# The output stage's orders, and head 0 of the expert retrieval by token tile with four modulation pieces on TensorE

## The chip, the cores and the metric

The kernel runs on one core of one Trainium2 chip. The metric is the device time of one execution in microseconds (us). The core has TensorE (PE in the rows, its weight loads PEld), VectorE (DVE), ScalarE (ACT), GpSimd (POOL) and SyncE (SP). Here SP issues the direct loads of weights and POOL the gathers and the loads of `w_ada`; 16 DMA engines carry both.

## The reference, cut to what matters

All in float32, 256 tokens of width 2048 (two token tiles of 128):

```python
mod = silu(c) @ w_ada + b_ada                 # w_ada: 2048 x 12288, six parts of 2048
sh1, sc1, g1, sh2, sc2, g2 = split(mod, 6)
...                                           # attention: stick-breaking heads and latent heads
mixed = concat(norm(sb_out), norm(mla_out)) @ w_o
x = x + g1 * mixed
h2 = rmsnorm(x, norm2_g) * (1 + sc2) + sh2
q = h2 @ w_peer_q                             # 8 heads, two halves of 128 each
s1, s2 = q1 @ keys1.T, q2 @ keys2.T           # 128 scores a side, for each token and head
v1, i1 = top_k(s1, 16); v2, i2 = top_k(s2, 16)
best, pos = top_k(v1[:, None] + v2[None, :], 16)   # 16 experts of 16384
u, v = take(u_tab, expert), take(v_tab, expert)    # rows of 2048 numbers
x = x + g2 * sum(softmax(best) * gelu(u . h2) * v) # sum over 8 heads and 16 experts
return rmsnorm(x)
```

## The kernel before, in words

The kernel is written by hand: each engine has one program (`@block.tensor` and so on) that runs in its written order, and semaphores order the engines among each other. Memory is placed by hand too: `at(name, offset, shape)` puts a buffer at an address, and buffers whose lives don't overlap share one.

**Modulation.** `w_ada` comes in 96 pieces `k` of 1 MB (part `k // 16`, chunk `k % 16`). From piece 32 on POOL loads them (`ada_load`, L279) into three buffers `ada_late` in turn; each load waits until the piece that was in its buffer is summed. VectorE adds piece times `silu(c)` to `ada_acc` (`ada_sum`, L293). When the 16 pieces of a part are in, `ada_cols(part)` (L304) sums over the 128 partitions with 16 TensorE products that have one column each, and `ada_finish` adds the bias. The last three pieces go to buffers of their own (`ada_last`), which are loaded once the squares of the new `x` are done (`x2_squared`), ahead of pieces 89 to 92.

**Output stage.** `w_o` has four column groups `n`, each in 8 pairs `m` of chunks. For a pair ScalarE casts the weights to a high part (L416), VectorE makes the low part (L420), and TensorE runs 12 products of 512 columns (L927), the two token tiles `t` alternating. VectorE's list between these casts holds `ada_sum` of pieces 71 to 85, the residual sums, and in the last group the additions L1598 to L1607. `ada_cols(4)` stands behind pair 5 of group 2 on TensorE; the sum of piece 80 (pair 6) waits for it. Ahead of the stage ScalarE waits for the sums of squares of all 16 heads (L1233).

**Second norm and head 0.** x is normed, transposed (L946) and evicted to `h2T`. Then TensorE computes the queries `p{u}` of head `u` for both tiles at once: 32 products of 256 columns (L981), with weights `w_pq{u // 2}` from two slots (`ring`) of which each half is loaded when its last reader is done. `score(u)` (L958) makes the scores, ScalarE evicts them to `s_all`, and VectorE's `retrieve(part, q)` takes 17 parts to find the 16 experts of job `q` (token tile `q // 8`, head `q % 8`). `token_rows(u)` (L967) transposes `h2T` back to rows `h2`. `ada_cols(5)` stands in head 2 behind pair 5.

**Experts.** There are 256 slots `n` (job `n // 16`). POOL gathers for each slot a row of `peer_u` per token (1 MB) into seven `u_rows`, and later, between them, a row of `peer_v` into nine `v_rows`. VectorE's `serve(n)` is the product `dot(n)` (L1740) and, behind it, a share of the retrieval of a later job: jobs 1 and 2 over slots 0 to 7 and 8 to 15, then job `q + 2` over the 16 slots of job `q`. TensorE sums the `v_rows` in PSUM (L1012). What holds the first gathers, in POOL's order:

```python
if n % TOPK == 0: pool.wait_ge(experts_ready, n // TOPK + 1)
if n < 3:   pool.wait_ge(ada_steps, LAST_PIECES - EARLY)           # buffers of ada_late
elif n < 6: pool.wait_ge(ada_steps, LAST_PIECES - EARLY + n - 2)   # buffers of ada_last
if n == 6:  pool.wait_ge(ada_columns, 4)                           # ada_acc, after ada_cols(5)
```

From slot 7 on a gather of `u` waits for the product seven slots back. The gather of `v` 0 waits for `p5` and that of `v` 4 for `p7`, whose weights lay where the `v_rows` are.

## Time and profile before

| | us |
|---|---|
| median of 3 runs | 1834.54 (1834.16 to 1836.43) |
| the profiled execution | 1835.33 |
| its span in the trace | 1832.7 |
| TensorE, busy | 1473.0 (80%) |
| VectorE, busy | 1141.4 (62%) |
| ScalarE, busy | 349.0 (19%) |
| GpSimd, busy | 619.3 (34%) |

The page splits the span into 40 slices of 45.8 us. Experts fill it from slice 12 on. Times in the rows are us from the start of the span. Matmuls in float32 show as two records each, so that "x32" at L304 is 16 products.

### The profile page before, as it was taken

The page shows a single profiled execution, that of the slowest core. Times are in us where ns is not written, and L with a number is a line of the kernel's source. Part 1 is how long each engine was busy: PE and PEld are TensorE (multiplying, and loading weights), DVE is VectorE, ACT ScalarE, POOL GpSimd, SP SyncE. Part 2 cuts the span into 40 slices and gives each one's busy share as a digit, 9 for nine tenths or more (in the row PEclk, how much of TensorE's full clock was granted, in tenths as well). Part 3 has the DMA queues.
Part 4 walks back from the last instruction along what each step waited for, and adds up shares of the span by engine and source line. Part 5 has one row for each costly group of instructions (what it writes and reads, how often), then busy time and mean ns, then how long its engine had stood idle before and what let it go on. Part 6 is the DMA issues. An engine that isn't in the chain of part 4 may idle for free.

```text
span 1832.7 us, 13707 instructions
## 1 busy us (share of the span) xinstructions
PE 1473.0 (80%) x4834; PEld 829.5 (45%) x4834; DVE 1141.4 (62%) x1562; ACT 349.0 (19%) x697; POOL 619.3 (34%) x625
## 2 busy tenths in 40 slices
PE   2979999899898987777777777778777777777776
PEld 2559986887787632232322323224332322232332
DVE  5868786788789855545455555538555555544445
ACT  3004342852301211011110100102111101010110
POOL 0001111001064863444334343418543443433341
PEclk9989999999999999999999999998999999999999
DMA  9999998569799999999999999999999999999995
GB/s 340 386 388 405 400 353 313 204 238 384 273 360 413 421 422 421 422 422 422 422 421 422 422 422 421 422 421 404 421 422 423 422 422 422 422 422 421 422 421 233
DMA packets 138241, 716.43 MB, mean 391 GB/s; under 512 B 11158, under 2 KB 15436, under 8 KB 63692
## 3 DMA queue, kind: packets, MB, share of 16 engines
q0 software_dynamic: 82976, 604.02, 79.8%
q1 hardware_dynamic: 55212, 111.77, 16.6%
q8 instruction: 25, 0.41, 0.1%
q14 instruction: 28, 0.23, 0.0%
HBM read 713.65 MB, written 2.10 MB: 391 GB/s over the span
## 4 chain that ended last, share of the span: by engine, by line
DMA 60%; PE 18%; DVE 11%; POOL 5%; issue 3%; ACT 2%; SPq 1%; DVEq 0%; POOLq 0%; ACTq 0%
DMA u_rows<-in_peer_u,expert 49%; PE ps L981 4%; PE ps L768 4%; DMA v_rows<-in_peer_v,expert 4%; DVE u_rows L1740 3%; DVE first_acc L454 3%; POOL v_rows L665 3%; DMA ring<-in_w_peer_q 2%; PE ps L762 2%; POOL u_rows L665 2%; DMA ada_first<-in_w_ada 2%; PE ps L927 2%; DMA ada_late<-in_w_ada 2%; DVE ada_acc L293 1%; DMA u_rows<-in_peer_v,expert 1%
## 5 line engine op out<-in xcount | busy, mean ns | idle before, releaser
L1012 PE MATMUL ps<-v_rows,diag 128*128 128x512 f32 x1960 | 902.5, 606 | 271.5 <-DMA v_rows<-in_peer_v,expert 257.4
L1740 DVE SCALAR_TENSOR_TENSOR u_rows<-u_rows,h 128x2048 f32<-128x2048 f32 x256 | 587.0, 2293 | 519.8 <-DMA u_rows<-in_peer_u,expert 517.3
L1012 PEld LDWEIGHTS ps<-v_rows,diag 128*128 128x128 f32 x1960 | 357.5, 191 | 815.1 <-issue 586.3
L665 POOL DMA_INDIRECT u_rows<-in_peer_u,expert x256 | 286.0, 1117 | 620.9 <-DVE u_rows L1740 574.8
L665 POOL DMA_INDIRECT v_rows<-in_peer_v,expert x249 | 285.3, 1146 | 97.3 <-issue 78.3
L1339 ACT ACTIVATE diag<-ident,hidden 128x128 f32<-128x128 f32 x250 | 89.3, 395 | 846.8 <-PE ps L1012 532.9
L293 DVE SCALAR_TENSOR_TENSOR ada_acc<-ada_late,cact,ada_acc 128x2048 f32<-128x2048 f32 x57 | 133.9, 2349 | 18.2 <-DMA ada_late<-in_w_ada 17.1
L279 POOL DMA_DIRECT2D ada_late<-in_w_ada x61 | 32.3, 530 | 314.1 <-DVE ada_acc L293 268.3
L981 PE MATMUL ps<-h2T,ring 128*128 128x256 f32 x512 | 117.5, 390 | 6.4 <-DMA ring<-in_w_peer_q 6.4
L981 PEld LDWEIGHTS ps<-h2T,ring 128*128 128x128 f32 x512 | 99.4, 196 | 20.8 <-DMA ring<-in_w_peer_q 6.8
L454 DVE SCALAR_TENSOR_TENSOR first_acc<-ada_first,cact,first_acc 128x1024 f32<-128x1024 f32 x60 | 77.0, 1284 | 15.1 <-DMA ada_first<-in_w_ada 9.6
L732 PE MATMUL ps<-opened,hT 128*128 128x512 f32 (+1 forms) x128 | 53.5, 581 | 5.8 <-DVE hT L1447 5.8
L420 DVE TENSOR_TENSOR ring_low<-ring,win_high 128x1024 fp32r<-128x1024 f32 x40 | 48.0, 1220 | 13.4 <-ACT win_high L416 13.3
L416 ACT CAST win_high<-ring 128x1024 fp32r<-128x1024 f32 x40 | 41.6, 1051 | 74.7 <-DMA ring<-in_w_in 39.3
L927 PE MATMUL ps<-wo_high,mix_high_part 128*128 128x512 f32 x128 | 42.1, 411 | 7.3 <-DVE ring_low L420 7.2
L927 PE MATMUL ps<-wo_high,mix_low_part 128*128 128x512 f32 x128 | 41.7, 409 | 0.0
L646 POOL MEMSET kpad<- 128x512 f32 x1 | 0.5, 524 | 120.7 <-DVE a1c L1409 120.7
L732 PEld LDWEIGHTS ps<-opened,hT 128*128 128x128 f32 x128 | 26.9, 214 | 30.6 <-issue 26.2
L420 DVE TENSOR_TENSOR ring_low<-ring,wo_high 128x1024 fp32r<-128x1024 f32 x32 | 39.0, 1220 | 2.1 <-ACT wo_high L416 2.1
L416 ACT CAST wo_high<-ring 128x1024 fp32r<-128x1024 f32 x32 | 33.5, 1048 | 31.7 <-PE ps L927 31.7
L1287 ACT ACTIVATE hidden<-hidden 128x16 f32<-128x16 f32 x16 | 3.5, 216 | 173.1 <-DVE u_rows L1740 173.0
L927 PE MATMUL ps<-ring_low,mix_high_part 128*128 128x512 f32 x128 | 35.5, 401 | 0.0
(273 smaller groups left out, 1262.6 us busy)
## 6 DMA issues: line engine op xcount, KB each, us to landing
ada_late<-in_w_ada POOLq DMA_DIRECT2D x61, 1024.0 KB, 7.9
ada_first<-in_w_ada SPq DMA_DIRECT2D x64, 512.0 KB, 11.6
ring<-in_w_in SPq DMA_DIRECT2D x10, 2048.0 KB, 25.6
ring<-in_w_o SPq DMA_DIRECT2D x8, 2048.0 KB, 20.5
ring<-in_w_peer_q SPq DMA_DIRECT2D x8, 2048.0 KB, 14.4
opened<-in_w_in SPq DMA_DIRECT2D x8, 1024.0 KB, 12.8
u_rows<-in_peer_u,expert POOLq DMA_INDIRECT x256, 32.2
v_rows<-in_peer_v,expert POOLq DMA_INDIRECT x249, 34.2
```

What stands on the lines that cost most here:

```text
L293: nc.vector.scalar_tensor_tensor(out=a, in0=piece, scalar=cact[:, kc:kc + 1], in1=a, op0=ALU.mult, op1=ALU.add).then_inc(ada_steps, 1)
L416: nc.scalar.copy(self.high, self.whole).then_inc(made, 1)
L420: nc.vector.tensor_tensor(self.low, self.whole, self.high.bitcast(F32), ALU.subtract).then_inc(done, 1)
L454: nc.vector.scalar_tensor_tensor(out=a, in0=piece, scalar=cact[:, kc:kc + 1], in1=a, op0=ALU.mult, op1=ALU.add).then_inc(first_steps, 1)
L665: nc.gpsimd.indirect_dma_start(buf[:, :], None, table, bass.IndirectOffsetOnAxis(ap=expert[:, q, k:k + 1], axis=0)).then_inc(done, 16)
L732: ins = nc.tensor.matmul(banks[name][t][:, 0:width], hT[:, ch, P * t:P * t + P], w[:, ch % 4, 0:width], start=(ch == 0), stop=last)
L768: ins = nc.tensor.matmul(banks[b // 2][:, T * (b % 2):T * (b % 2) + T], w.of(part, k, P * b, P), h[:, ch, :], start=first and b % 2 == 0, ...
L927: ins = nc.tensor.matmul(banks[t], mixed[:, h, P * t:P * t + P], w.of(part, k), start=first, stop=last)
L981: ins = nc.tensor.matmul(bank[:, T * s:T * s + T], ring[item[name][0]][:, lo:lo + P], h2T[:, ch, :], start=(ch == 0 and s == 0), stop=(ch ...
L1012: ins = nc.tensor.matmul(ps[:, c, :], diag[i % len(diag)][:, :], buf[:, 512 * c:512 * c + 512], start=(n % HALF_SLOTS == 0), stop=last)
L1339: nc.scalar.activation(diag[i % len(diag)][:, :], ident[:, :], ACT.Copy, scale=hidden[:, q % 4, k:k + 1]).then_inc(diagonal, 1)
L1740: nc.vector.scalar_tensor_tensor(out=buf[:, :], in0=buf[:, :], scalar=1.0, in1=h2[:, q // H, :], op0=ALU.mult, op1=ALU.mult, accum_out=hid ...
```

## The change

1. **Orders of the output stage.** ScalarE's load of the activation table ahead of attention moves up behind the copies `uq`. The wait for all sums of squares ahead of the output stage goes; the casts of `mix` wait each for its own heads, the last for the sums. VectorE's first step on these sums moves behind pair 1. `ada_cols(4)` moves from behind pair 5 to behind pair 3 of group 2. The last pair runs tile 0 and then tile 1.
2. **Head 0 by token tile.** `first_head(t)` computes the queries of one tile with tokens as rows: 16 products of 256 columns. They are copied to `q0`, transposed (`first_turned`), copied and scored (`first_score`), so that VectorE can retrieve job 0 when tile 0 alone is scored.
3. **Four pieces on TensorE.** `ada_last` has four buffers (pieces 92 to 95) on one semaphore. They are not summed by VectorE: `last_piece(i)` multiplies each with its column of `silu(c)` right into the PSUM columns of part 5. `ada_cols(5)` adds the rest to them and moves to the end of head 1.
4. **Buffers and retrievals.** `u_rows` 0 to 2 lie where `ada_last` 1 to 3 were, 3 to 5 at `ada_late`, 6 at `ada_acc`; the waits of the first gathers follow. VectorE retrieves job 0 behind the sum of piece 88, waits until POOL has issued the first gather, then sums pieces 89 to 91. Job 2 and all later ones are spread over 16 slots from slot 8 on.

```diff
-    LAST_PIECES = 6 * KC - 3
+    LAST_PIECES = 6 * KC - 4
+    def last_piece(i):
+        if i == 0:
+            nc.tensor.wait_ge(ada_last_loaded, 16 * len(ada_last))
+        k = LAST_PIECES + i
+        part, kc = divmod(k, KC)
+        for b in range(KC):
+            ins = nc.tensor.matmul(ps[:, 7, KC * part + b:KC * part + b + 1], ada_last[i][:, P * b:P * b + P],
+                                   cact[:, kc:kc + 1], start=(i == 0 and b == 0), stop=False, skip_group_check=True)
+        ins.then_inc(ada_columns, 1)
...
                 if n < 3:
-                    pool.wait_ge(ada_steps, LAST_PIECES - EARLY)
+                    pool.wait_ge(ada_columns, 5 + n)
                 elif n < 6:
-                    pool.wait_ge(ada_steps, LAST_PIECES - EARLY + n - 2)
+                    pool.wait_ge(ada_steps, LAST_PIECES - EARLY - 5 + n)
                 if n == 6:
-                    pool.wait_ge(ada_columns, 4)
+                    pool.wait_ge(ada_columns, 8)
...
+                    if w.c == 4 * PAIRS - 1:
+                        for t in range(TT):
+                            for p in products:
+                                product(*p, t)
...
-                    if n == 2 and m == 5:
+                    if n == 2 and m == 3:
                         ada_cols(4)
...
+            first_head(0, 0, KC)
+            first_head(1, 0, 3)
+            first_turned(0)
+            first_head(1, 3, 6)
+            first_score(0)
+            first_head(1, 6, KC)
+            last_piece(0)
+            first_turned(1)
+            last_piece(1)
+            first_score(1)
+            last_piece(2)
+            last_piece(3)
+            for u in range(4):
+                token_rows(u)
-            for u in range(H):
+            for u in range(1, H):
...
-                    if u == 2 and m == 5:
+                    if u == 1 and m == 7:
                         ada_cols(5)
...
-            act.wait_ge(squares_summed, JOBS)
             for n in range(4):
                 for m in range(PAIRS):
                     if n == 0:
+                        copied(act, f"o{4 * m + 2 if 2 * m < H else 4 * m + 3 - 2 * H}")
+                        if m == PAIRS - 1:
+                            act.wait_ge(squares_summed, JOBS)
...
-                job, slots = (1 + k // 8, 8) if q == 0 else (q + 2, TOPK)
+                job, slots, k2 = (1, 8, n) if n < 8 else (2 + (n - 8) // TOPK, TOPK, (n - 8) % TOPK)
...
-            for k in g2_steps[:-3]:
+            for k in g2_steps[:3]:
                 ada_sum(k)
             for part in range(RETRIEVAL):
                 retrieve(part, 0)
-            for k in g2_steps[-3:]:
+            dve.wait_ge(first_issued, 1)
+            for k in g2_steps[3:-4]:
                 ada_sum(k)
```

TensorE's order from the transposes of the second norm on, before: head 0 in one (32 products), its rows and scores, head 1, and `ada_cols(5)` (L304) in head 2.

```order
L946 MATMUL ps<-ident,xs_116 128x128 x32
L981 MATMUL ps<-h2T,ring_49 128x256 x32
L967 MATMUL ps<-ident,h2T 128x128 x4
L958 MATMUL ps<-kT,pq 128x128 x4
L967 MATMUL ps<-ident,h2T 128x128 x12
L981 MATMUL ps<-h2T,ring_49 128x256 x32
L981 MATMUL ps<-h2T,ring_50 128x256 x4
L958 MATMUL ps<-kT,pq 128x128 x4
L981 MATMUL ps<-h2T,ring_50 128x256 x20
L304 MATMUL ps<-ones,ada_acc 128x1 x16
```

The same place now; L317 is `last_piece`.

```order
L969 MATMUL ps<-ident,xs_117 128x128 x32
L1003 MATMUL ps<-ring_49,h2T 128x256 x19
L1012 MATMUL ps<-ident,q_188 128x128 x2
L1003 MATMUL ps<-ring_49,h2T 128x256 x3
L1019 MATMUL ps<-kT,pq 128x128 x2
L1003 MATMUL ps<-ring_49,h2T 128x256 x10
L317 MATMUL ps<-cact,ada_last_88 128x1 x16
L1012 MATMUL ps<-ident,q_188 128x128 x2
L317 MATMUL ps<-cact,ada_last_89 128x1 x16
L1019 MATMUL ps<-kT,pq 128x128 x2
L317 MATMUL ps<-cact,ada_last_90 128x1 x16
L317 MATMUL ps<-cact,ada_last_91 128x1 x16
```

Four times 16 products with one column stand now between head 0 and the token rows, and with them ahead of head 1.

POOL's order from the loads of `ada_last` to the eighth gather, with the waits, before:

```order
L279 DMA ada_last_88<-in_w_ada 128x2048 [waits x2_squared]
...
L665 DMA u_rows_134<-in_peer_u,expert 128x2048 [waits ada_steps,experts_ready]
L665 DMA u_rows_135<-in_peer_u,expert 128x2048 [waits ada_steps]
L665 DMA u_rows_136<-in_peer_u,expert 128x2048 [waits ada_steps]
...
L665 DMA u_rows_140<-in_peer_u,expert 128x2048 [waits ada_columns]
L665 DMA u_rows_134<-in_peer_u,expert 128x2048 [waits dots]
```

and now:

```order
L281 DMA ada_last_88<-in_w_ada 128x2048 [waits x2_squared]
...
L679 DMA u_rows_135<-in_peer_u,expert 128x2048 [waits ada_columns,experts_ready]
L679 DMA u_rows_136<-in_peer_u,expert 128x2048 [waits ada_columns]
L679 DMA u_rows_137<-in_peer_u,expert 128x2048 [waits ada_columns]
...
L679 DMA u_rows_141<-in_peer_u,expert 128x2048 [waits ada_columns]
L679 DMA u_rows_135<-in_peer_u,expert 128x2048 [waits dots]
```

The first three gathers wait no longer for VectorE's sums but each for one `last_piece` on TensorE.

## Rows read from the trace of the kernel before

**Rows 1.** The page: rate of the DMA engines in 40 slices.

```profile
GB/s 340 386 388 405 400 353 313 204 238 384 273 360 413 421 422 421 422 422 422 422 421 422 422 422 421 422 421 404 421 422 423 422 422 422 422 422 421 422 421 233
```

**Rows 2.** Stretches: window, length, busy us (PE, PEld, DVE, ACT, POOL), clock, DMA share, GB/s.

```profile
500.00:505.00 5.00, 5.00 (x26) 4.44 (x25) 4.33 (x19) 0.59 (x1) 0.00 (x0) 1.00 0.01 3
505.00:510.00 5.00, 5.00 (x25) 4.40 (x24) 4.39 (x16) 0.00 (x0) 0.00 (x0) 1.00 0.19 59
...
520.00:600.00 80.00, 73.58 (x356) 64.69 (x355) 73.57 (x134) 10.22 (x19) 43.78 (x29) 0.91 1.02 415
```

**Rows 3.** Timeline of POOL, first and seventh gather; idle before and releaser in brackets.

```profile
510.84 2.88 POOL L665 DMA_INDIRECT u_rows<-in_peer_u,expert  x1 [17.42 <-DVE expert L1713]
...
529.98 0.94 POOL L665 DMA_INDIRECT u_rows<-in_peer_u,expert  x1 [5.81 <-PE ps L304]
```

**Rows 4.** Timeline of TensorE: head 0, and from head 1 into head 2.

```profile
481.38 14.05 PE L981 MATMUL ps<-h2T,ring 128*128 128x256 f32 x64
...
500.25 15.71 PE L981 MATMUL ps<-h2T,ring 128*128 128x256 f32 x72
```

**Rows 5.** Timeline of VectorE: three sums, start of retrieval 0, first product.

```profile
482.36 7.25 DVE L293 SCALAR_TENSOR_TENSOR ada_acc<-ada_late,cact,ada_acc 128x2048 f32<-128x2048 f32 x3
...
500.52 0.29 DVE L1672 MAX8 tk_v<-s_all 128x8 f32<-128x128 f32 x1
...
518.58 2.29 DVE L1740 SCALAR_TENSOR_TENSOR u_rows<-u_rows,h 128x2048 f32<-128x2048 f32 x1 [0.83 <-DMA u_rows<-in_peer_u,expert]
```

**Rows 6.** Chain that ended last: three pairs, `ada_cols(4)`, load of piece 85, `ada_cols(5)`.

```profile
422.89 8.45 PE ps L927 x36
431.34 3.48 PE ps L304 x32
...
443.30 9.12 DMA ada_late<-in_w_ada
...
525.49 4.22 PE ps L304 x32
```

**Rows 7.** Stretches of 1 us (columns as in Rows 2) in and behind these products.

```profile
432.00:433.00 1.00, 1.00 (x12) 1.00 (x11) 0.00 (x0) 1.00 (x2) 0.00 (x0) 1.00 1.05 387
436.00:437.00 1.00, 1.00 (x4) 0.81 (x3) 1.00 (x2) 0.00 (x0) 0.50 (x1) 0.50 1.05 387
527.00:528.00 1.00, 1.00 (x11) 1.00 (x10) 1.00 (x1) 0.00 (x0) 0.00 (x0) 1.00 1.10 440
528.00:529.00 1.00, 1.00 (x7) 1.00 (x6) 1.00 (x3) 0.00 (x0) 0.00 (x0) 0.50 0.88 358
534.00:535.00 1.00, 1.00 (x4) 0.82 (x3) 0.71 (x2) 0.00 (x0) 0.70 (x2) 0.59 0.96 393
```

**Rows 8.** Timelines of VectorE and TensorE in the output stage.

```profile
434.92 1.29 DVE L290 TENSOR_SCALAR ada_acc<-ada_late,cact 128x2048 f32<-128x2048 f32 x1 [4.45 <-PE ps L304]
...
434.67 0.72 PE L927 MATMUL ps<-wo_high,mix_high_part 128*128 128x512 f32 x2
...
438.97 0.76 PE L927 MATMUL ps<-wo_high,mix_high_part 128*128 128x512 f32 x2
...
456.07 0.98 PE L927 MATMUL ps<-wo_high,mix_high_part 128*128 128x512 f32 x2 [2.05 <-DVE ring_low L420]
...
469.55 1.04 PE L908 MATMUL ps<-ident,knat 128*128 128x128 f32 x8
```

**Rows 9.** Timeline of ScalarE: start of attention, start and end of the output stage.

```profile
309.96 1.28 ACT L1205 ACT_TABLE_LOAD   x1
...
360.78 0.62 ACT L1237 CAST mix_high_part<-mix 128x512 fp32r<-128x512 f32 x1 [0.39 <-PE ps L886]
...
472.49 0.63 ACT L1230 ACTIVATE junk<-x 128x512 f32<-128x512 f32 x1 [0.60 <-DVE x L1607]
```

**Rows 10.** Timelines: VectorE at the start of attention; POOL's gather of `v` 4.

```profile
310.83 2.35 DVE L293 SCALAR_TENSOR_TENSOR ada_acc<-ada_late,cact,ada_acc 128x2048 f32<-128x2048 f32 x1 [0.42 <-DMA ada_late<-in_w_ada]
...
619.92 2.42 POOL L665 DMA_INDIRECT v_rows<-in_peer_v,expert  x1 [0.56 <-PE ps L981]
```

More of the change, by code:

```diff
@@ L310, in ada_finish @@
     def ada_finish(part):
-        nc.vector.wait_ge(ada_columns, part - 1)
+        nc.vector.wait_ge(ada_columns, part - 1 if part < 5 else 8)
         lo, hi = KC * part, KC * part + KC
@@ L366, in build @@
     before_retrieval = list(used)
-    plan([f"p{u}" for u in range(8)], [0, 1, 2, 3])
-    plan([f"sc{u}" for u in range(8)], [4, 5])
+    plan(["fq_0", "fq_1", "p0_0", "p0_1"] + [f"p{u}" for u in range(1, 8)], [0, 1, 2, 3])
+    plan(["sc0_0", "sc0_1"] + [f"sc{u}" for u in range(1, 8)], [4, 5])
     plan([f"h2_{u}" for u in range(8)], [6])
@@ L661, in _, with gather @@
                 ada_load(pool, k)
-            def gather(n, buf, done, table):
+            def gather(n, buf, done, table, issued=None):
                 q, k = divmod(n, TOPK)
-                nc.gpsimd.indirect_dma_start(buf[:, :], None, table,
-                                             bass.IndirectOffsetOnAxis(ap=expert[:, q, k:k + 1], axis=0)).then_inc(done, 16)
+                nc.gpsimd.indirect_dma_start(buf[:, :], None, table, bass.IndirectOffsetOnAxis(ap=expert[:, q, k:k + 1], axis=0),
+                                             engine_sem=issued).then_inc(done, 16)
             def gather_u(n):
@@ L968, in token_rows, with first_head, first_turned, first_score @@
                 fill(ins, f"h2_{u}")
-            for u in range(H):
+            w0 = ring[item["w_pq0"][0]][:, :].rearrange("p (kc n) -> p kc n", kc=KC)
+            def first_head(t, lo, hi):
+                if lo == 0:
+                    take(pe, f"fq_{t}")
+                for ch in range(lo, hi):
+                    if t == 0 and ch % 2 == 0:
+                        copied(pe, f"h2T{ch // 2}")
+                    if t == 0 and ch % KH == 0:
+                        loaded(pe, "w_pq0", ch // KH)
+                    ins = nc.tensor.matmul(ps[:, unit[f"fq_{t}"][0], 0:2 * P], h2T[:, ch, P * t:P * t + P], w0[:, ch, 0:2 * P],
+                                           start=(ch == 0), stop=(ch == KC - 1))
+                if hi == KC:
+                    fill(ins, f"fq_{t}")
+            def first_turned(t):
+                copied(pe, f"fq_{t}")
+                bank = take(pe, f"p0_{t}")
+                for s in range(2):
+                    ins = nc.tensor.transpose(bank[:, P * s:P * s + P], q0[:, t, P * s:P * s + P], ident[:, :])
+                fill(ins, f"p0_{t}")
+            def first_score(t):
+                copied(pe, f"p0_{t}")
+                bank = take(pe, f"sc0_{t}")
+                for s in range(2):
+                    ins = nc.tensor.matmul(bank[:, P * s:P * s + P], pq[:, 0, s, P * t:P * t + P], kT[:, H * s, :], start=True, stop=True)
+                fill(ins, f"sc0_{t}")
+            first_head(0, 0, KC)
[13 more added lines that the diff above has]
+            for u in range(1, H):
                 name, bank = f"w_pq{u // 2}", take(pe, f"p{u}")
                 for m in range(PAIRS):
-                    if u == 0:
-                        copied(pe, f"h2T{m}")
                     if u % 2 == 0 and m % (PAIRS // 2) == 0:
@@ L1298, in std, with first_query, first_query_turned, first_scores_out @@
                 nc.scalar.activation(st[:, 2 + t:3 + t], st[:, 2 + t:3 + t], ACT.Sqrt).then_inc(y_std, 1)
-            for u in range(H):
+            def first_query(t):
+                empty(nc.scalar.copy(q0[:, t, :], full(act, f"fq_{t}")[:, 0:2 * P]), f"fq_{t}")
+            def first_query_turned(t):
+                empty(nc.scalar.copy(pq[:, 0, :, P * t:P * t + P], full(act, f"p0_{t}")[:, 0:2 * P].rearrange("p (s t) -> p s t", s=2)),
+                      f"p0_{t}")
+            def first_scores_out(t):
+                if t == 1:
+                    act.wait_ge(ada_columns, 4)
+                empty(nc.scalar.copy(s_all[:, t, 0:2, :], full(act, f"sc0_{t}")[:, 0:2 * P].rearrange("p (s n) -> p s n", s=2)),
+                      f"sc0_{t}")
+            first_query(0)
+            first_query_turned(0)
+            first_scores_out(0)
+            first_query(1)
+            first_query_turned(1)
+            first_scores_out(1)
+            for u in range(4):
+                token_rows_out(u)
+            for u in range(1, H):
                 if u == 4:
@@ L1304, in _ @@
                 query(u)
-                if u == 0:
-                    token_rows_out(0)
                 scores_out(u)
-                if u == 0:
-                    for k in range(1, 4):
-                        token_rows_out(k)
                 if u == 4:
@@ L1719, in retrieve @@
                 t, h = divmod(q, H)
-                if part == 0 and t == 0:
-                    copied(dve, f"sc{h}")
+                if part == 0 and (t == 0 or h == 0):
+                    copied(dve, f"sc{h}" if h else f"sc0_{t}")
                 if part < 8:
@@ L1785, in serve @@
                     ada_finish(5)
-                job, slots = (1 + k // 8, 8) if q == 0 else (q + 2, TOPK)
+                job, slots, k2 = (1, 8, n) if n < 8 else (2 + (n - 8) // TOPK, TOPK, (n - 8) % TOPK)
                 if job < QJOBS:
-                    for part in range(RETRIEVAL * (k % slots) // slots, RETRIEVAL * (k % slots + 1) // slots):
+                    for part in range(RETRIEVAL * k2 // slots, RETRIEVAL * (k2 + 1) // slots):
                         retrieve(part, job)
```

68 lines of the change are left out of this document (35 added, 33 removed).

## The prediction, made before the changed kernel was run

> **What bounds the kernel now.** I read the page's slices first: from slice 12 to the end the DMA engines are full at 421 to 422 GB/s [rows 1]. The 512 gathers of 1 MB (2.49 us each at 421 GB/s) and the late weight loads fill 1300 us without a gap; the stretch 520 to 600 already runs at 415 GB/s [rows 2]. The bytes don't change. So the end moves only by DMA time that was empty and is now used, or was used and is now empty. I read next the stretches just ahead: 3 and 59 GB/s from 500 to 510 [rows 2]. This hole is there because nothing can be issued: POOL sits 17.42 us until the experts of job 0 are found [rows 3], and the next query weights wait for head 1.
>
> Call S the start of head 0's products, 481.4 now [rows 4]. VectorE starts retrieval 0 at S+19.1 and its first product at S+37.2 [rows 5]; POOL has the experts and issues its first gather at S+29.5 and the seventh, held by `ada_cols(5)`, at S+48.6 [rows 3]. The query weights of slot 0 are read half way through head 1, S+18.9+7.0=S+26 [rows 4], so DMA is full again from about S+27.7 and stays so.
>
> **The change part by part.**
>
> *Table load: 0.* Its 1.28 us at 309.96 stand in ScalarE's path [rows 9], but VectorE, which takes the next step, sums a piece until 313.1 [rows 10]; the piece's load covers it. Without this cover it would be worth up to 1.3.
>
> *Wait for the squares: -0.4.* The cast at 360.78 sat 0.39 for TensorE [rows 9]; now it follows ScalarE's own step. The lower bound of the gain is 0, were the new waits as late.
>
> *`ada_cols(4)`: -4.3.* VectorE sat 4.45 for it [rows 8], and the low parts behind were late: TensorE waited 2.05 at 456.07. From 422.89 on TensorE has 13 pairs of 2.82 (8.45 for three), 3.48 for the columns [rows 6] and 1 for eight of the keys' transposes, 41.1 in all. About 1.2 more goes to the half clock behind the columns: 436 to 437 shows it at 0.50 [rows 7], and the pair from 434.67 to 438.97 took 4.3 [rows 8]. So it ends its last pair at 465.2 instead of 469.5 [rows 8]. Ends: -3, if the loads of the pieces, which land 9.1 behind their issue [rows 6], hold VectorE as they did; -6, if small waits within the 8.45 go too.
>
> *Tile 0 first in the last pair: -0.6.* VectorE gets tile 0 six products (1.4) earlier, but ScalarE is behind with the copies of the keys; of its way to the last square only the idle 0.60 ahead of 472.49 goes [rows 9].
>
> Together S comes 5.2 earlier, at 476.2 (ends 3.5 and 7).
>
> *Head 0 by tile.* 32 products cost 14.05, 0.44 each [rows 4]; 16 cost 7.0. Tile 0's queries are there at S+7, turned at S+8.6, scored at S+10.4 and evicted at S+10.9, with three products of tile 1 in each gap to hide the copies. VectorE is done with three sums (7.25) at S+8.3 [rows 5]. Retrieval takes 10.0 (500.5, with POOL released at 510.5 or just behind [rows 3, 5]), so experts are ready at S+21, 8 earlier. That is the gain meant. What is late next? The first gather needs the buffer of `last_piece(1)`, and the second and third those of pieces 2 and 3.
>
> *The pieces on TensorE.* Each is 16 one-column products, as `ada_cols` is: 3.48 at full clock [rows 6]. Tile 1 ends at S+14.8, piece 0 at S+18.3. Then comes the clock. Behind the L304 products at 431.2 it was 0.50 at 436; at 528, with TensorE busy all of every microsecond and 2.7 into the L304 products, it fell from 1.00 to 0.50; 534 to 535, in ordinary products since 529.7, is the first stretch above that again (0.59) [rows 7]. These are the levels 2.4 and 1.2 GHz. The stint that straddled the fall took 4.22 instead of 3.48 [rows 6]: 7 records a us instead of 11 or 12. Four pieces in a row are four such stints, so from the second on I take twice 3.48. Pieces 1, 2 and 3 then end at S+25.3, S+33.2 and S+40.2 (at full clock S+22.1, S+25.8 and S+29.3).
>
> Here a rule of the Trainium skill speaks against my reading: "TensorE: Matmul & The Clock Gate", section "What's actually happening", has the clock set by how busy the engine has been, low by default and full when busy. By it pieces that keep TensorE fully busy stay at full clock. The rows at 527 to 529 speak against it, for a busy engine with one-column products; what it would give is the first rival.
>
> *Behind the pieces.* Token rows 0 to 3, now behind all pieces, take about as long as the 4.8 between head 0 and head 1 now [rows 4], 6 at half clock: S+46. VectorE's first product needs them, so it starts at S+46 instead of S+37. Head 1 takes 14.05 and some 2.5 for the clock: S+62.5. Then `ada_cols(5)`: S+66, and only then POOL's seventh gather, which was issued at S+48.6. And VectorE behind its first product wants the scores of head 1 for retrieval 1; these come in head 2, at about S+71. Before they were there before the first product. POOL's eighth gather needs that one product, its ninth the second: so from S+49 to S+75 VectorE stands.
>
> *What DMA does with it.* Transfers begin some 1.5 behind the issue. Gather 0: S+27.7, just as before. It takes 2.5, then DMA is empty until gather 1 at S+35.6 (5.4 lost) and gather 2 at S+42.6 (4.5). Gathers 2 to 5 last until S+52.6; half a load of query weights comes at S+56.5 (3.9), the next with the end of head 1 at S+64 (2.5). Gathers 6 and 7 follow; from 8 on each waits for a product. A slot costs VectorE 2.3 and an eighth of a retrieval, 3.6, against 2.5 of DMA: some 6 slots lose 1 each before the last query weights fill the holes, less what the queue holds. I take 5 (2 to 10). Sum: 5.4+4.5+3.9+2.5+5=21.
>
> *Retrievals over 16 slots.* Job 2 costs VectorE half as much per slot from slot 8 on (0.6 instead of 1.25). Later in steady state VectorE has room; 0.
>
> *Gather 0 with VectorE silent.* 0.94 instead of 2.88 for its issue [rows 3]; in the times above.
>
> *Sum*, against the profiled execution: 1835.3-5.2+21=1851. It lies 0.8 above the median, within what a chip adds; I leave it.
>
> **The rivals.**
>
> *Full clock* (the rule above). Gathers 0 to 2 at S+24.5, S+28.2 and S+31.8 lose 1.2 and 1.1, the query weights 1.3 and 2.1, VectorE's pace 4; the phase starts 3.1 earlier: 9.7-3.1=+6.6. 1835.3-5.2+6.6=1837. For it: the L304 stint at 431 ran at 1.00 to its end. Against: the one at 525 did not, and these are four times as long.
>
> *Faster: the intended outcome.* At full clock, with TensorE never late behind: the queued gathers and weights bridge VectorE's wait for head 1, nothing is lost from head 1 on but the three first holes (3.6), and the output stage gives 6.6. 1835.3-6.6-3.1+3.6=1829. It decides when head 1's scores come less than some 10 us behind the first product, since POOL has seven buffers. Against it: gather 6 waits for `ada_cols(5)`, at S+52 even then, and is in order ahead of all others.
>
> *Slower still.* TensorE reaches `p7` late and POOL's gather of `v` 4, which waits for it, stands while the queue runs dry; before it waited just 0.56 at S+138.5 [rows 10], so there is little to spare, and `p7` would be some 20 later, at S+160. Priced at 8 more: 1859.
>
> **How the numbers follow.** Forecast 65%, with its own range 1845 to 1858; full clock 17%; faster 11%; slower still 7%. The range that leaves out no more than 2 in 10 runs from 1834 (the full clock with its terms 3 better) to 1858. About 0.2% (3.7 us) is what a measurement of this kernel can tell from no change. Faster by more than that (under 1830.9) has 0.12, within it 0.16, slower 0.72.
>
> **What would show each step.** In the changed profile: S near 476, and TensorE's last L927 product ending near 465. Experts at S+21 and the first gather released not by VectorE's `expert` but by TensorE's L317. Clock 0.50 in the stretches behind the first `last_piece`, and each later piece near 7; at 1.00 and 3.5 the forecast is wrong and the first rival right. The gathers 0, 1, 2 some 7 apart with DMA below 250 GB/s between S+30 and S+42. VectorE idle 20 us behind its first product, released by the eviction of head 1's scores; gather 6 released by L304 near S+66. DMA from S+95 on at 421 as before: any other rate there would upset the whole argument.

## The result, and the profile after

The changed kernel takes **1846.76 us** (median of 5 runs, 1843.04 to 1849.69) against 1834.16 (5 runs, 1833.11 to 1836.43) for the kernel before, measured beside it: **1.0067 times the time, 95% interval 1.0053 to 1.0082**, slower by 12.6 us. The profiled execution of it took 1845.27 us with a span of 1842.9; before, 1835.33 and 1832.7.

The page's slices, first the granted clock of TensorE in tenths, then the rate of the DMA engines:

```profile
PEclk8989999999889999999999999998999999999999
...
GB/s 339 386 390 404 397 351 321 185 265 389 259 288 393 412 421 422 422 422 421 422 422 421 422 421 422 422 422 413 422 422 423 422 422 422 421 422 421 422 422 236
```

Against [rows 1] the slices 10 to 12, counted from 0 (461 to 599 us), are lower: 259, 288 and 393 where 273, 360 and 413 stood. Slice 13 has 412 for 421, and from slice 14 on both kernels move 421 to 423 in all but one slice and the last. So next to nothing was lost in the 1200 us of gathers; it was lost between 484 and 574 us.

TensorE's timeline from the last products of the output stage to head 1's scores (start, length, engine, line, out<-in, count of records, idle before and releaser in brackets):

```profile
474.29 8.39 PE L1003 MATMUL ps<-ring,h2T 128*128 128x256 f32 x38
...
488.80 3.63 PE L317 MATMUL ps<-cact,ada_last 128*128 128x1 f32 x32
...
492.54 5.66 PE L317 MATMUL ps<-cact,ada_last 128*128 128x1 f32 x32
...
499.05 13.65 PE L317 MATMUL ps<-cact,ada_last 128*128 128x1 f32 x64
512.57 1.09 PE L990 MATMUL ps<-ident,h2T 128*128 128x128 f32 x4
...
518.83 15.12 PE L1046 MATMUL ps<-h2T,ring 128*128 128x256 f32 x64
533.78 3.63 PE L306 MATMUL ps<-ones,ada_acc 128*128 128x1 f32 x32
...
539.94 1.86 PE L981 MATMUL ps<-kT,pq 128*128 128x128 f32 x8
```

S, the start of head 0's products, is 474.3 (481.38 before [rows 4]). The first piece takes 3.6 us, the second 5.7, the last two 6.8 each. Head 1 begins at S+44.5; before it began at S+18.9 [rows 4].

POOL's timeline, the gathers that waited:

```profile
499.07 1.00 POOL L679 DMA_INDIRECT u_rows<-in_peer_u,expert  x1 [15.55 <-PE ps L317]
506.15 2.06 POOL L679 DMA_INDIRECT u_rows<-in_peer_u,expert  x1 [6.08 <-PE ps L317]
512.98 0.94 POOL L679 DMA_INDIRECT u_rows<-in_peer_u,expert  x1 [4.77 <-PE ps L317]
...
537.68 0.94 POOL L679 DMA_INDIRECT u_rows<-in_peer_u,expert  x1 [20.05 <-PE ps L306]
```

The experts were there at 495.1, S+20.8. The first gather went out at S+24.8, the second and third each some 7 us later, the seventh at S+63.4. In [rows 3] the first one waited for VectorE's `expert` and the seventh was issued at S+48.6.

VectorE's timeline: the experts, its first product of rows, and its wait for head 1's scores.

```profile
494.96 0.17 DVE L1791 SCALAR_TENSOR_TENSOR expert<-tk_f 128x16 uint32<-128x16 f32 x1
...
519.76 2.29 DVE L1818 SCALAR_TENSOR_TENSOR u_rows<-u_rows,h 128x2048 f32<-128x2048 f32 x1 [12.40 <-ACT h L1339]
...
542.45 0.29 DVE L1750 MAX8 tk_v<-s_all 128x8 f32<-128x128 f32 x1 [20.39 <-ACT s_all L1335]
```

Stretches from S on (columns as in [rows 2]), first of the changed kernel, S+28 to S+100:

```profile
474.00:502.00 28.00, 28.00 (x160) 26.30 (x157) 19.08 (x42) 3.25 (x8) 2.59 (x4) 0.85 0.58 230
502.00:519.00 17.00, 14.97 (x68) 13.77 (x68) 5.16 (x3) 1.75 (x3) 5.80 (x5) 0.50 0.55 196
519.00:534.00 15.00, 15.00 (x68) 13.03 (x66) 2.30 (x2) 0.60 (x2) 0.00 (x0) 0.93 0.82 318
534.00:549.00 15.00, 15.00 (x82) 13.65 (x82) 6.25 (x13) 1.15 (x2) 2.81 (x3) 0.89 0.84 300
549.00:574.00 25.00, 25.00 (x127) 22.24 (x126) 23.80 (x47) 2.93 (x5) 7.11 (x8) 1.00 0.99 368
```

and the same stretches, as seen from S, of the kernel before:

```profile
481.00:509.00 28.00, 26.35 (x133) 22.70 (x132) 25.01 (x43) 4.32 (x8) 2.11 (x4) 1.00 0.52 201
509.00:526.00 17.00, 17.00 (x88) 15.14 (x87) 14.02 (x16) 1.18 (x2) 11.80 (x6) 1.00 1.02 389
526.00:541.00 15.00, 15.00 (x72) 13.30 (x72) 12.84 (x25) 1.17 (x2) 9.80 (x5) 0.77 1.02 415
541.00:556.00 15.00, 15.00 (x77) 13.32 (x76) 14.17 (x30) 1.76 (x3) 8.26 (x7) 1.00 1.02 414
556.00:581.00 25.00, 25.00 (x127) 22.12 (x127) 23.88 (x42) 4.62 (x10) 15.38 (x8) 1.00 1.02 412
```

I turn a rate into **idle** time: the stretch times (1 - rate/421). After: 12.7, 9.1, 3.7, 4.3 and 3.1 us; before: 14.6, 1.3, 0.2, 0.2 and 0.5. With the last 26 us (0.4 and 0.2) that is 33.3 against 17.1, 16.2 us more.

Two lengths within one execution leave out that the output stage starts a few us earlier or later from one execution to the next (418 to 424 us in those profiled). **Stage**: from the product that ends the chain's last long wait, one pair or three ahead of `ada_cols(4)`, to S; in both kernels that is pair 3 of group 2. The chain has it at

```profile
422.19 3.06 PE ps L939 x12
425.25 3.46 PE ps L306 x32
428.71 31.69 PE ps L939 x132
```

so 52.1 us; before, 422.89 [rows 6] to 481.38 is 58.5. **Rest**: from S to the end of the span, 1842.9-474.3=1368.6; before, 1832.7-481.4=1351.3. The change is -6.4 in the stage and +17.3 in the rest (the stage began 0.7 earlier besides), and the 17.3 are the 16.2 us of empty DMA engines and the 1 us of the slice behind (412 for 421).

### The profile page after: what moved, and what is told of

Its sections match the earlier page's. It is cut to its first block, busy times and chain, and to the rows that moved or that the text cites. A ratio compares the mean times of both kernels' runs of the same rounds, so it can differ in the third digit from the quotient of the medians.

```text
span 1842.9 us, 13978 instructions
## 1 busy us (share of the span) xinstructions
PE 1496.9 (81%) x4966; PEld 852.6 (46%) x4966; DVE 1132.1 (61%) x1558; ACT 349.7 (19%) x701; POOL 627.6 (34%) x625
## 3 DMA queue, kind: packets, MB, share of 16 engines
q1 hardware_dynamic: 55212, 111.77, 16.5%
## 4 chain that ended last, share of the span: by engine, by line
DMA 57%; PE 15%; DVE 12%; POOL 9%; issue 4%; ACT 2%; SPq 2%; DVEq 0%; POOLq 0%; ACTq 0%
DMA u_rows<-in_peer_u,expert 47%; POOL u_rows L679 5%; DVE u_rows L1818 4%; POOL v_rows L679 4%; DMA v_rows<-in_peer_v,expert 4%; PE ps L939 3%; DVE first_acc L467 2%; PE ps L776 2%; DMA ring<-in_w_in 2%; PE ps L782 2%; DVE ada_acc L295 1%; DMA ada_first<-in_w_ada 1%; DMA u_rows<-in_peer_v,expert 1%; PE ps L317 1%; PE ps L438 1%
## 5 line engine op out<-in xcount | busy, mean ns | idle before, releaser
L679 POOL DMA_INDIRECT u_rows<-in_peer_u,expert x256 | 289.7, 1132 | 632.8 <-DVE u_rows L1818 561.7
L679 POOL DMA_INDIRECT v_rows<-in_peer_v,expert x249 | 289.9, 1164 | 97.2 <-issue 78.8
L295 DVE SCALAR_TENSOR_TENSOR ada_acc<-ada_late,cact,ada_acc 128x2048 f32<-128x2048 f32 x56 | 131.5, 2348 | 22.2 <-DMA ada_late<-in_w_ada 16.1
L1046 PE MATMUL ps<-h2T,ring 128*128 128x256 f32 x448 | 100.8, 385 | 0.0
L1046 PEld LDWEIGHTS ps<-h2T,ring 128*128 128x128 f32 x448 | 85.6, 193 | 11.4
L433 DVE TENSOR_TENSOR ring_low<-ring,win_high 128x1024 fp32r<-128x1024 f32 x40 | 48.0, 1219 | 13.8 <-ACT win_high L429 13.8
```

Source lines behind the costliest of these rows:

```text
L295: nc.vector.scalar_tensor_tensor(out=a, in0=piece, scalar=cact[:, kc:kc + 1], in1=a, op0=ALU.mult, op1=ALU.add).then_inc(ada_steps, 1)
L433: nc.vector.tensor_tensor(self.low, self.whole, self.high.bitcast(F32), ALU.subtract).then_inc(done, 1)
L679: nc.gpsimd.indirect_dma_start(buf[:, :], None, table, bass.IndirectOffsetOnAxis(ap=expert[:, q, k:k + 1], axis=0), engine_sem=issued).the ...
L1046: ins = nc.tensor.matmul(bank[:, T * s:T * s + T], ring[item[name][0]][:, lo:lo + P], h2T[:, ch, :], start=(ch == 0 and s == 0), stop=(ch ...
```

## The experiments

In three groups on two chips, each beside the kernel before (medians 1835.0, 1835.3 and 1834.5): `e1` to `e4` on one chip, `e5` to `e8` on another, `e9`, `e10` and `a1` on the first again. Ratios are to the kernel before of the same group. Only the third group has the changed kernel in it too. The columns: S of the profiled execution, the rest, the start of head 1's products and of its scores counted from S, and the idle DMA time of the first 126 us from S, as above.

```
                    median  ratio  95% interval     S     rest   head 1 scores  idle
kernel before         -     1         -           481.4  1351.3   18.9   34.4   17.1
changed kernel      1846.8  1.0067 1.0053-1.0082  474.3  1368.6   44.5   65.6   33.3
a1_changed_again    1844.8  1.0053 1.0040-1.0067  474.1  1371.9   45.0   69.4   36.8
e1_orders           1828.5  0.9969 0.9957-0.9981  470.1  1351.7   18.9   34.4   15.6
e2_head0            1851.6  1.0090 1.0075-1.0106  482.4  1368.6   45.2   66.5   34.5
e3_tile_vector      1828.4  0.9963 0.9951-0.9975  475.2  1355.2   21.1   36.6   19.3
e7_tile_five        1828.1  0.9962 0.9949-0.9975  478.8  1351.3   21.0   36.5   16.6
e4_pieces_one       1823.5  0.9940 0.9926-0.9954  474.7  1347.6   22.2   43.4   12.1
e5_pieces_half      1831.4  0.9982 0.9973-0.9991  473.5  1358.3   31.2   55.6   23.0
e9_one_piece        1826.2  0.9952 0.9939-0.9965  477.4  1349.7   25.5   46.7   15.0
e10_pieces_apart    1845.1  1.0063 1.0051-1.0075  472.4  1369.3   30.7   65.8   33.6
e6_retrieve_later   1845.4  1.0049 1.0036-1.0062  475.2  1368.9   44.9   69.3   31.9
e8_cols_early       1842.7  1.0038 1.0023-1.0052  475.6  1364.8   44.6   66.5   29.2
```

Times from S are of one execution each. The rest of the changed kernel differs by 3.3 us between its two profiled executions (1368.6 and 1371.9), so a difference of 3 or 4 us between two rests shows nothing by itself. With the new orders the stage took 52.0 to 52.3 us in all profiled executions but those of `e7_tile_five` and `e9_one_piece` (54.6 and 54.4).

**Do the two parts add up?** The kernel before with the orders alone, and the changed kernel with the orders undone:

```diff
+                    if w.c == 4 * PAIRS - 1:
+                        for t in range(TT):
+                            for p in products:
+                                product(*p, t)
-                    if n == 2 and m == 5:
+                    if n == 2 and m == 3:
                         ada_cols(4)
```

> The kernel before with the output stage's orders alone: the early table load, the wait for the squares put behind the first copies, ada_cols(4) in front of the last two products' pairs, and the last pair by token tile. Head 0, the sums of the pieces and the retrievals stay as before. Theory (two parts that add up: orders gain, head 0 loses): head 0 starts some 6.9 us earlier, as it did in the changed kernel (474.45 for 481.38), and nothing behind it gives that back, so 1834.2 - 6.9 = 1827 us (1826 to 1829). Rival 1 (the earlier start meets transfers that are not there yet, and the DMA queues idle as much longer in head 0 and 1 as the stage got shorter): 1832 to 1835 us. Rival 2 (most of the 6.9 us came only together with the pieces being taken off VectorE): 5.3 us, as I had summed it, or less: 1829 to 1832 us.

> The changed kernel with the output stage's orders undone: head 0 by token tile, the last four pieces on TensorE, the re-placed retrievals. Theory: this part alone carries the whole loss, 17 us in the two profiled executions (9.9 + 6.9) and 19.5 by the medians (12.6 + 6.9): 1851 to 1854 us, with the clock at 0.50 in the pieces as before. Rival (the two parts don't add up: the loss comes only where the earlier start of head 0 leaves too little loaded, so that undoing the orders costs little or nothing): 1844 to 1848 us.

Measured: 0.9969 and 1.0090, that is -5.7 and +16.5 us by the ratios (the medians: -6.5 and +16.6). Together +10 to +11; the whole change gave 1.0067 and, in its second measurement, 1.0053, 12.3 and 9.7 us. They add up, and neither needs the other: the rival in which the orders gain nothing is out, and so is the one in which undoing them costs little (1844 to 1848). TensorE's chain in the orders alone is the changed kernel's:

```profile
418.05 3.01 PE ps L925 x12
421.07 3.46 PE ps L304 x32
424.53 31.67 PE ps L925 x132
457.08 2.75 PE ps L925 x12
```

From 418.05 to S at 470.09 are 52.0 us; with the orders undone, 424.20 to 482.35, 58.2.

**What in the second part costs?** The last four pieces back on VectorE, with head 0 still by token tile. The lines below leave out that `ada_cols(5)` goes back to head 2, that VectorE no longer waits for the first gather, and that piece 91 is loaded behind the third gather.

```diff
-            last_piece(0)
             first_turned(1)
-            last_piece(1)
             first_score(1)
-            last_piece(2)
-            last_piece(3)
...
+            order = (86, 87, 92, 93, 94, 95, 88, 89, 90, 91)
+            for i, k in enumerate(order[:4]):
+                ada_sum_after(k, 54 + i)
             for part in range(RETRIEVAL):
                 retrieve(part, 0)
+            for i, k in enumerate(order[4:]):
+                ada_sum_after(k, 58 + i)
```

> The changed kernel with the last four pieces back on VectorE, in the order 86, 87, 92, 93, first retrieval, 94, 95, 88 to 91, and ada_cols(5) back in head 2; the orders of the output stage and head 0 by token tile stay, and so do the places of the retrievals. Theory (TensorE at half clock in the one-column products is what holds the gathers and head 1): all of it goes, the experts of the first tile stand at about 21 us behind the start of head 0 where the kernel before had 29, head 1 ends some 20 us earlier than in the changed kernel; the loss of 17 us goes, and up to 5 us of the idle that the kernel before had around its own first gathers goes too: 1822 to 1828 us, most likely 1825. Rival 1 (head 0 by token tile or the places of the retrievals carry the loss, by VectorE's wait for head 1's scores between two retrievals): 1835 to 1845 us. Rival 2 (four sums of 1.1 us each back on VectorE, at the time when it has the copies of head 0, hold back the scores): 1829 to 1834 us.

Measured 0.9963, 1828.4 us, between the theory's range and rival 2's: the loss is gone, so rival 1 (the order by tile or the places of the retrievals) is out. But of the 5 us on top none came. Two rows of it, VectorE and POOL, say why one part did not:

```profile
519.04 2.35 DVE L314 SCALAR_TENSOR_TENSOR ada_acc<-ada_late,cact,ada_acc 128x2048 f32<-128x2048 f32 x1 [8.08 <-DMA ada_late<-in_w_ada]
...
499.13 2.88 POOL L675 DMA_INDIRECT u_rows<-in_peer_u,expert  x1 [17.41 <-DVE expert L1787]
```

Piece 91 was loaded behind gathers and landed 8 us late. And the first gather stands at S+24.0, not S+21: VectorE's retrieval began at S+13.6 for S+10.8 in the changed kernel, since one sum more stands ahead of it and VectorE waited 3.18 us for the load of the pieces in `ada_last`. The second version loads no piece behind a gather:

```diff
-            order = (86, 87, 92, 93, 94, 95, 88, 89, 90, 91)
+            order = (86, 87, 88, 92, 93, 94, 95, 89, 90, 91)
```

> The kernel with the output stage's orders, head 0 by token tile and all last pieces on VectorE (1828.4 us), with the order of the pieces changed so that none is loaded behind gathers: 86, 87, 88, 92, 93, first retrieval, 94, 95, 89, 90, 91. In the former version piece 91 landed at 519 us, VectorE stood 8.1 us for it and the sixth gather stood 8.6 us. Theory (that stall held the transfers, 3 to 6 us): 1822 to 1826 us, below the orders alone. Rival (the first gather at 499 us sets the time in both, and what stands behind it is hidden by the weights of heads 2 and 3 that are transferred then): 1827 to 1829 us.

Measured 0.9962, as before: the rival. The stall was real, but whether it cost anything isn't shown: the rests differ by 3.9 (1355.2 against 1351.3), little more than two executions of one kernel, and the medians show no difference. Head 0 by token tile with everything on VectorE is worth no more than the orders alone (0.9963 and 0.9962 against 0.9969), though its first gather is issued at S+23.5 and not S+29.4. Three rows of the second version, POOL and two stretches, show why:

```profile
502.28 2.88 POOL L675 DMA_INDIRECT u_rows<-in_peer_u,expert  x1 [14.33 <-DVE expert L1783]
...
500.00:505.00 5.00, 5.00 (x25) 4.41 (x24) 4.67 (x6) 0.54 (x1) 2.72 (x1) 1.00 0.00 0
505.00:510.00 5.00, 5.00 (x25) 4.41 (x24) 4.79 (x3) 0.00 (x0) 4.39 (x3) 1.00 0.81 272
```

With VectorE summing beside it the issue takes 2.88 (1.00 in the changed kernel, where VectorE stood), so bytes move from about S+27. In the orders alone the hole ends at the same place, with the query weights that head 1, 2 us earlier from S, sets free: it moves 161 GB/s from 495 to 500, S+25 to S+30, ahead of its first gather. The hole is 14.0 and 13.5 us (idle from S to S+28). By these rows a gather issued 6 us earlier only takes the weights' place.

**The price of the products themselves**, with 1 and with 8 of 16 in each piece (the rest is left out of the computation):

```diff
-        for b in range(KC):
+        for b in range(1):
```

> The changed kernel with one of the 16 products in each of the four pieces that TensorE takes; 60 of the 64 one-column products are left out, so most of what the last four pieces add to the modulation is missing. All waits, transfers and orders stay. It prices the products themselves. Theory: about 22 us of TensorE between the end of head 0 and the token rows become 1.4 us, gathers follow one another at the pace of GpSimd and the transfers, head 1 starts 20 us earlier and runs at full clock: 1829 to 1834 us, that is 13 to 17 us under the changed kernel. Rival (the places of the retrievals among VectorE's work carry the loss, and the products are hidden beside them): 1842 to 1847 us.

> The changed kernel with 8 of the 16 products in each of the four pieces that TensorE takes (32 of the 64 one-column products are left out). With all 16 the four pieces took 22.3 us of TensorE and the kernel stood 23 us above the one with a single product in each (1823.5 us). Theory (the price of a product doubles once the clock has fallen to 0.50, and the clock falls some 5 us into such a stretch): the first piece costs 1.75 us at full clock, the second lies around the fall, the third and fourth cost 3.4 us each; 7 + 4 us of products where one product each was 1.4, token rows still at half clock: 1831 to 1835 us. Rival (a stretch half as long doesn't lose the clock): 7 us of products, token rows at 0.6 us each as at full clock, 1827 to 1830 us. Rival 2 (the whole price is the order of waits around the pieces and not their length): 1824 to 1826 us.

Measured 1823.5 and 1831.4. Theory holds for both, the first beyond its range: 21 to 23 us under the changed kernel, more than its whole loss. From 1 to 8 to 16 products head 1's start goes from S+22.2 to S+31.2 and S+44.5 (9.1 and 13.3 us) and the time from 1823.5 to 1831.4 and 1844.8 to 1846.8 (7.9 and 13.4 to 15.4). **In these three versions each us by which TensorE reached head 1 later cost about one.** Two things come later with it, the gathers that wait for pieces and the weights that wait for head 1; no version delays one without the other, so what each costs is not shown. The second half's products cost more each than the first's, 13.3/32=0.42 us for 9.1/28=0.32, most of them at half clock; stretches of the version with half the products:

```profile
485.00:490.00 5.00, 5.00 (x33) 4.61 (x32) 4.28 (x20) 0.37 (x1) 0.00 (x0) 1.00 0.56 229
490.00:495.00 5.00, 5.00 (x38) 5.00 (x37) 3.83 (x12) 0.74 (x2) 0.34 (x1) 0.77 0.00 0
495.00:500.00 5.00, 4.56 (x21) 4.16 (x21) 4.20 (x2) 0.40 (x1) 4.39 (x3) 0.50 0.70 233
```

Here too the clock fell, so the rival of a half as long stretch at full clock is out.

**Is it the length of the stretch?** The third and fourth piece moved among head 1's ordinary products:

```diff
-            last_piece(2)
-            last_piece(3)
...
+                    if u == 1 and m in (1, 3):
+                        last_piece(2 + m // 2)
```

> The changed kernel with two of its four pieces on TensorE moved among ordinary products: the third and fourth stand in head 1 behind its second and fourth block. As many one-column products, nothing left out; the second and third gather wait longer for their pieces. Theory (the stretch of one-column products is what costs: its second half ran at clock 0.50): the two moved pieces take 3.5 us each for 6.7, the token rows stand 13.4 us earlier, head 1 ends some 8 us earlier: 1838 to 1842 us for 1847. Rival 1 (the clock falls all the same behind the first two pieces and stays down through the token rows and head 1's first blocks): 1843 to 1846 us. Rival 2 (the second and third gather, 5 to 8 us later, take back what head 1 gains): 1846 to 1850 us.

Measured 1845.06, beside 1844.75 for the changed kernel in the same group: no gain, and the theory fell; rival 1's range (1843 to 1846) holds it. TensorE's timeline shows why head 1 gained nothing.

```profile
503.11 5.00 PE L1044 MATMUL ps<-h2T,ring 128*128 128x256 f32 x16
507.95 3.63 PE L317 MATMUL ps<-cact,ada_last 128*128 128x1 f32 x32
511.44 5.39 PE L1044 MATMUL ps<-h2T,ring 128*128 128x256 f32 x16
516.66 4.18 PE L317 MATMUL ps<-cact,ada_last 128*128 128x1 f32 x32
520.71 9.95 PE L1044 MATMUL ps<-h2T,ring 128*128 128x256 f32 x32
...
538.25 1.92 PE L981 MATMUL ps<-kT,pq 128*128 128x128 f32 x8
```

The two pieces are indeed nearly at their full-clock price (3.63 and 4.18, for 6.8), but the ordinary products now run in part at half clock. The first 16 records, ahead of the moved pieces, take 5.0, as the fall behind the first two pieces lasts until 505; the 16 and 32 behind the moved pieces take 5.4 and 9.95. The orders alone do 64 in 13.98 (3.5 and 7.0). Stretches of 1 us behind the first moved piece:

```profile
510.00:511.00 1.00, 1.00 (x12) 1.00 (x11) 0.00 (x0) 0.00 (x0) 0.00 (x0) 1.00 0.00 0
512.00:513.00 1.00, 1.00 (x6) 0.83 (x5) 0.00 (x0) 0.00 (x0) 0.82 (x1) 0.86 0.00 0
514.00:515.00 1.00, 1.00 (x3) 0.75 (x3) 0.00 (x0) 0.00 (x0) 0.00 (x0) 0.50 0.79 262
516.00:517.00 1.00, 1.00 (x8) 0.92 (x7) 0.00 (x0) 0.00 (x0) 0.00 (x0) 0.93 0.55 229
```

Here each of the three stints in head 1 (`ada_cols(5)` is the third) had its own fall a moment behind it. Head 1's scores come at S+65.8 as in the changed kernel. So setting the pieces apart did not save the clock's price; other products paid it. Head 1 began 13.8 us earlier than in the changed kernel and nothing was won, so its start alone does not set the time. Rival 2 is in the trace too: the second gather went out at S+39.4 for S+31.9 and the third at S+48.7 for S+38.7, and S+28 to S+45 has 12.7 us idle for 9.1, while the 30 us behind have 3.4 less. The run doesn't separate the two rivals.

**One piece in ten** on TensorE, the one whose buffer the first gather takes:

```diff
             first_head(1, 6, KC)
+            last_piece(1)
...
+            order = (86, 87, 88, 92, 94, 95, 89, 90, 91)
```

> The orders, head 0 by token tile, and one of the ten last pieces on TensorE (93, whose place the first gather takes), right behind head 0's products, where TensorE waits for copies anyway; VectorE sums 86, 87, 88, 92, first retrieval, 94, 95, 89, 90, 91. Nothing is left out. Theory (what costs is the length of the stretch of one-column products and not that they are on TensorE: one piece took 3.5 us at full clock): the first gather stands at 496 us for 499 in the version with all on VectorE (1828.3 us), and the queues idle that much shorter: 1824 to 1827 us. Rival (head 1 and the fall of the clock, 3.5 us and more behind the piece, take it back): 1828 to 1831 us.

Measured 0.9952, 1826.2 us, inside the theory's range and the fastest complete version here; against the orders alone (0.9969) and all on VectorE (0.9962) the intervals overlap, so it is at best 1 to 3 us and may be nothing. The first gather stands at 498.53, S+21.2, for S+23.5 in the version with all on VectorE; VectorE's list ahead of the retrieval has one sum less. Its piece took 3.63, and the clock fell behind it all the same: token rows 1.1 us each for 0.66, the first 64 records of head 1 in 16.07. Its head 1 begins 4.5 us later than with all on VectorE and the scores come 10 us later, and it is no slower: here, where the gathers follow one another from the first on, a late head 1 cost nothing that the medians show.

**The wait of VectorE for head 1's scores**, and the seventh gather's:

```diff
-                job, slots, k2 = (1, 8, n) if n < 8 else (2 + (n - 8) // TOPK, TOPK, (n - 8) % TOPK)
-                if job < QJOBS:
+                job, slots, k2 = (1, 4, n - 4) if n < 8 else (2 + (n - 8) // TOPK, TOPK, (n - 8) % TOPK)
+                if job < QJOBS and n >= 4:
```

> The changed kernel with one thing moved: the parts of head 1's first retrieval stand in VectorE's slots 4 to 7 (behind four products of gathered rows) and not in slots 0 to 7. Nothing is left out. It prices my fifth term: VectorE stood 20.4 us between its first product and head 1's scores while rows that had landed waited. Theory (the gathers from the eighth on wait for those products, so the queues idle some 5 us for it): 1.0067 x 1835 = 1847 without the move, 1841 to 1843 with it. Rival (the seventh gather is what stands, and it waits for ada_cols(5) behind head 1's products, so the products of rows are hidden): 1846 to 1848 us.

> As the version with the retrieval in slots 4 to 7, and ada_cols(5), for whose result the seventh gather waits, in head 1 behind the second block of products and not behind the eighth; it is some 11 us earlier. Nothing is left out. Theory (the transfers of 520 to 545 us, 322 GB/s, stand because of the seventh gather, which waited 20.05 us for it): another 3 to 6 us less than the retrieval's move alone, 1836 to 1840 us. Rival (by then the queues carry the weights of heads 2 and 3 that have to be transferred anyway, and the gathers only change places with them): as the retrieval's move alone, within 1 us.

Measured 1.0049 for the first (1845.4 us, between the theory's range and the rival's), against 1.0067 and 1.0053 for the changed kernel in other groups: 1 to 3 us, within the error. Its POOL rows give the rival's reason: the seventh gather went out at 541.35 after 22.39 of idle time, released by `ada_cols(5)`. The products that VectorE had done by then let the ninth to the twelfth follow at 1.25 us distance (in the changed kernel the ninth stood 6.22), but all of them stand behind the seventh. With `ada_cols(5)` earlier too the seventh goes out at 528.60 and the time is 1.0038 (1842.7 us), 3 to 5 us under the changed kernel: less than I had expected of the two together (7 to 11). Beside the retrieval's move alone in the same group it is 2 to 3 us, more than the rival's 1 and less than the theory's 3 to 6, and the intervals overlap; `ada_cols(5)` earlier by itself was not run. POOL then stood 10.18 ahead of the thirteenth gather, for a product that VectorE did at 545 us, behind the first parts of head 1's retrieval: the wait for head 1's scores again.

The changed kernel again, as the base of the third group:

> The changed kernel itself, beside the two versions above on one chip, as their common base. Both theories: 1845 to 1849 us, 1.0067 times the kernel before.

It gave 1844.8, just under its range. The changed kernel's two measurements differ by 0.14%; across groups the rows of the table can't be compared more finely than that.

## Why the prediction was right, step by step

The sign, the mechanism and the range held: 1846.76 for 1851.0. By its own steps:

- **Output stage, -5.2.** Measured -6.4 (58.5 to 52.1), in three parts. Up to the last product of the stage it is -4.8, where I had -4.3: VectorE's idle 4.45 went and of TensorE's 2.05 all but 0.4, and the half clock behind the columns (0.50 from 430 to 432), for which I had kept 1.2, cost 0.7 (11 pairs in 31.69 us, for eleven times 2.82). From there to the first transpose it is -0.7, for the -0.6 of the last pair. The transposes themselves gave 0.9, which I did not have: the clock was 0.96 in their first us (469 to 470), where before it was 0.50 from the first on (475 to 480). The -0.4 of the wait for the squares lies ahead of this length, and no run has it alone.
- **Experts at S+21**: S+20.8. **Pieces** ended at S+18.3, 25.3, 33.2 and 40.2 by the forecast; TensorE ended them near S+18.1, 23.9 and 38.4 (the last two in one row, 6.8 each). The rule of the Trainium skill ("TensorE: Matmul & The Clock Gate", section "What's actually happening"), by which a busy engine gets the full clock, gave my first rival, 1837; here TensorE was busy all of 484 to 512 and ran at 0.50 for most of it, so by that rule, read as busy time alone, the trace does not agree.
- **Seven us between the gathers 0, 1 and 2**: 7.1 and 6.8. The two holes, 9.9 by the forecast, are 7.8 us more idle than before in S+28 to S+45.
- **Token rows until S+46**: first product at S+45.5. **Head 1 until S+62.5**: S+59.7, as the clock cost 1.1 in it and not 2.5 (in the second measurement's profile it cost 2.4). **Seventh gather at S+66**: S+63.4. **Scores at S+71**: S+65.6.
- **VectorE stands from S+49 to S+75**: it stood, S+47.8 to S+68.2. Idle beyond S+60 is 6.9 us more than before, where I had 2.5 (end of head 1) and **5 for VectorE's pace**, 7.5 in all; between S+45 and S+60 it is 3.5, for 3.9. Together the terms hold, but how the 7.5 divide is not shown, and 5 for VectorE looks too much: with its wait moved away 1 to 3 us came back, within the error, since the seventh gather stood as before; with `ada_cols(5)` earlier too it was 3 to 5.
- **The first hole.** I took its end as unchanged; it is 1.9 shorter, since the changed kernel's loads of pieces keep the queues at 424 GB/s up to S+10 (474 to 484), where before the ten us from S had 310.
- **Sum of the ledger**: 21 by the forecast, 16.2 by the stretches, 17.3 by the rest. The forecast lies 5.7 us above the profiled execution: 3.7 here, 1.2 in the stage and 0.7 by which the stage began earlier. The median of the five runs is 1.5 above the profiled one, so against it the error is 4.2.
- **Full clock** (1837): the clock fell, as said above. **Slower still** by `p7`: POOL shows no wait for TensorE between 600 and 700; it did not come in. **Faster**: its condition (scores within 10 us of the first product) was missed by 10.

## What to carry over

Where empty transfer time sets the end, ask of each instruction put ahead of the next issuer's release what it holds back, even on an engine with idle time: here 60 one-column products cost 21 to 23 us of the end. The whole change let the experts come 8 us earlier, and 6 of these were there with all pieces on VectorE too. Price a step that sheds work from one engine by the amount: one piece on TensorE, where TensorE waited anyway, gained 1 to 3 us at best; four lost 16 to 19 against none. And measure parts of a combined change alone: this one held 6 us of gain that the other part hid.

## What the runs showed of the hardware

In the pieces the granted clock fell from 1.00 to 0.50 while TensorE was busy without a gap (in the changed kernel 1.00 from 485 to 490, 0.88 to 495 and 0.50 to 510, with 5.00 busy in each 5 us), and the products behind paid as well as those within: in the version with the pieces apart the first moved piece ran at 1.00, and the clock was 0.86 and then 0.50 in the ordinary products from 512 to 516.

A stint of 16 one-column products was not always followed by a fall. Behind `ada_cols(5)` the clock went to 0.50 in the changed kernel (539 to 541) and in the version with the pieces apart (534 to 540), but in the version with one product in each piece it stayed at 1.00, and so it did in the version with one piece (522 to 537) and with the orders undone (542 to 557). Of the version with one product in each piece, within this stint and behind it:

```profile
514.00:515.00 1.00, 1.00 (x12) 1.00 (x11) 0.00 (x0) 0.00 (x0) 0.00 (x0) 1.00 1.06 438
...
517.00:518.00 1.00, 1.00 (x7) 0.87 (x6) 0.00 (x0) 0.00 (x0) 0.70 (x2) 1.00 1.03 403
```

The same version had lost the clock at 494, with 4 one-column products in all ahead of the token rows, while the version without any, with the same token rows, had not:

```profile
494.00:495.00 1.00, 0.74 (x4) 0.62 (x4) 0.93 (x2) 0.21 (x1) 0.00 (x0) 0.70 0.00 0
...
494.00:495.00 1.00, 0.59 (x4) 0.42 (x4) 0.85 (x5) 0.36 (x1) 0.00 (x0) 1.00 0.00 0
```

The first row is of the version with one product in each piece, the second of that with none. What decides between these cases the runs leave open.
